# Taking a norm's root out of the matmul operand and multiplying it in on evacuation

## The reference, cut to what matters

```python
def rms_norm(x, w):
    return x * lax.rsqrt(jnp.mean(x * x, axis=-1, keepdims=True) + EPS) * w

def swiglu(x, w_gate, w_up, w_down):
    return (silu(x @ w_gate) * (x @ w_up)) @ w_down      # 1024 -> 2816 -> 1024

x = x + 0.5 * swiglu(rms_norm(x, ffn1_norm), ...)        # stage f1
h = rms_norm(x, mix_norm)
proj = h @ w_in                                          # conv inputs, gates, decay, q, k, v
x = x + concat([gdn_mixer(...), dilated_mixer(...)]) @ w_out
x = x + 0.5 * swiglu(rms_norm(x, ffn2_norm), ...)        # stage f2
x = rms_norm(x, final_norm)
```

## Time and profile before

| what | value |
|---|---|
| three runs | 2655.34, 2647.42, 2653.19 us; median 2653.19 us |
| the profiled execution | 2648.88 us, span 2647.0 us |
| PE matmul busy | 2557.2 us, 97% of the span |
| DVE busy | 1669.7 us, 63% |
| ACT busy | 1102.4 us, 42% |
| first block | about the first 665 us |

### The profile page before, as it was taken

One profiled execution on the slowest core, in us unless ns is written; L12 is line 12 of the kernel. 1 busy time (PEld: TensorE's weight loads), 2 busy tenths in 40 slices (PEclk: granted clock), 3 DMA queues, 4 the chain that ended last, 5 costly groups with the idle time before them and its releaser, 6 DMA issues.

```text
span 2647.0 us, 38421 instructions
## 1 busy us (share of the span) xinstructions
PE 2557.2 (97%) x15704; PEld 2268.5 (86%) x15704; DVE 1669.7 (63%) x2645; ACT 1102.4 (42%) x1728; POOL 64.4 (2%) x60
## 2 busy tenths in 40 slices
PE   7998898999999999999999999999999999998998
PEld 7998798999888888778888888889888888888998
DVE  6767644777677655666644767755555446776655
ACT  5445654555322223444243422224222225755553
POOL 0001031000000000000100000000000000000000
PEclk9999999999999999999999999999999999999999
DMA  7765201675455442212222455543444323244554
GB/s 261 233 231 184 88 17 62 208 240 185 167 180 185 168 150 97 66 40 80 94 90 88 143 187 177 176 163 111 145 140 134 135 98 126 89 138 149 179 189 148
DMA packets 109536, 379.92 MB, mean 144 GB/s; under 512 B 11952, under 2 KB 15792, under 8 KB 108976
## 3 DMA queue, kind: packets, MB, share of 16 engines
q1 hardware_dynamic: 108352, 372.80, 42.2%
q10 hardware_dynamic: 1008, 4.65, 0.5%
HBM read 376.36 MB, written 1.05 MB: 143 GB/s over the span
## 4 chain that ended last, share of the span: by engine, by line
PE 89%; DVE 5%; ACT 3%; issue 2%; DMA 0%; ACTq 0%; DVEq 0%
PE B L1499 26%; PE B L1501 26%; PE B L1500 26%; DVE w_lo L2129 2%; ACT w_hi L1820 1%; PE B L1760 1%; PE B L1743 1%; PE B L1514 1%; PE B L1653 1%; PE B L1515 1%; PE B L1516 1%; PE B L1666 1%; PE B L1750 1%; DVE AC L2374 1%; DVE TMP L2156 0%
## 5 line engine op out<-in xcount | busy, mean ns | idle before, releaser
L1499 PE MATMUL B<-U,w_hi 128*128 128x256 f32 (+1 forms) x2896 | 958.8, 331 | 7.9 <-DVE w_lo L2129 7.8
L1500 PE MATMUL B<-U,w_hi 128*128 128x256 f32 (+1 forms) x2896 | 950.7, 328 | 0.0
L1501 PE MATMUL B<-U,w_lo 128*128 128x256 f32 (+1 forms) x2896 | 950.5, 328 | 0.0
L2129 DVE TENSOR_TENSOR w_lo<-w_raw,w_hi 128x1024 fp32r<-128x1024 f32 (+3 forms) x583 | 683.2, 1184 | 385.6 <-ACT w_hi L1820 384.8
L1820 ACT ACTIVATE w_hi<-w_raw 128x1024 fp32r<-128x1024 f32 (+3 forms) x583 | 589.4, 1017 | 494.6 <-PE B L1501 471.9
L1499 PEld LDWEIGHTS B<-U,w_hi 128*128 128x128 f32 x2896 | 546.3, 189 | 64.4 <-issue 7.5
L1500 PEld LDWEIGHTS B<-U,w_hi 128*128 128x128 f32 x2896 | 546.1, 189 | 52.6 <-issue 1.5
L1501 PEld LDWEIGHTS B<-U,w_lo 128*128 128x128 f32 x2896 | 546.1, 189 | 51.6
L1499 PE MATMUL B<-HHf,w_hi 128*128 128x256 f32 (+1 forms) x1122 | 363.9, 324 | 1.5 <-DVE w_lo L2129 1.5
L1500 PE MATMUL B<-HLf,w_hi 128*128 128x256 f32 (+1 forms) x1122 | 363.0, 324 | 0.0
L1501 PE MATMUL B<-HHf,w_lo 128*128 128x256 f32 (+1 forms) x1122 | 363.0, 324 | 0.0
(11 more groups left out here) (360 smaller groups left out, 2510.1 us busy)
## 6 DMA issues: line engine op xcount, KB each, us to landing
w_raw<-in_w SPq DMA_DIRECT2D x504, 512.0 KB, 4.2
w_ada<-in_w SPq DMA_DIRECT2D x144, 512.0 KB, 3.3
w_raw<-in_w SPq DMA_DIRECT2D x58, 384.0 KB, 3.2
w_raw<-in_w SPq DMA_DIRECT2D x8, 320.0 KB, 2.8
X<-in_x SPq DMA_DIRECT2D x2, 1024.0 KB, 9.6
w_raw<-in_w SPq DMA_DIRECT2D x8, 256.0 KB, 2.7
BW<-in_bias ACTq DMA_DIRECT2D x1, 1536.0 KB, 10.2
CN<-in_consts ACTq DMA_DIRECT2D x1, 1152.0 KB, 5.3
```

The source lines that it names most:

```text
L1499: pe.matmul(o, hi, xh, start=i == 0 and s.start, stop=False)
L1500: pe.matmul(o, hi, xl, start=False, stop=False)
L1501: e = pe.matmul(o, lo, xh, start=False, stop=i == last and s.stop)
L2129: dve.tensor_tensor(w_lo[:, plan.slot[u], 0:n], w_raw[:, plan.ring[u], 0:n], w_hi[:, plan.slot[u], 0:n].bitcast(F32), ALU.subtract).then_i ...
```

## The change

In the first block no normed state is made. A step `raw` writes `hi` and `lo` of X times the norm's weight as soon as a chunk of X is final (at the start: as soon as it has landed), so the products read that. The root is one number for each token, so it can be multiplied in behind the products: on the gate bank ahead of silu (`g_r`), on the down product ahead of `x_add` (`x_r`; the up product is linear, so its root waits until there), on each bank of `mix1` as it is evacuated (`conv_in`, `gate_in`, `decay_tr`, `qk_sq`, now on VectorE), and for v, whose tokens lie on partitions, through a transposed root (`r_tr`) as the scale of ScalarE's copy. A `pair` behind a norm is cut in half, and the sum over partitions and the root stand between the halves. At the start X is loaded in two halves, with the first weight unit between them.

```diff
-                while done < min(at + AHEAD + 1, len(cut)) and ...
+                while done < min(at + (s.n if s.kind == "fetch" and s.n else AHEAD + 1), len(cut)) and ...
+    def raw(self, name, k, *need):
+        self.add("raw", key=(name, k), x=self.view, need=need)
+    def raw_begin(self, name, keys, wts, stat):
+        need = tuple(("ul", ("raw", name, k)) for k in range(8))
+        b, b2 = self.PS.get(), self.PS.get()
+        f = dict(x=self.view, n=256, need=need, b=b, b2=b2)
+        self.add("pair", key=(), wts=wts[:8], **f)
+        rb = stat.rsqrt(D)
+        self.add("pair", key=keys, wts=wts[8:], k0=4, **f)
+        self.lastU = ("mm", keys[1])
+        self.add("ahead")
+        return rb, dict(zip(keys, (b, b2)))
...                                                  # ffn, down part
-            self.x_add((p, "d", m), n, b, gate)
+            self.x_add((p, "d", m), n, b, gate, rb=rb)
             stat.add_("X", m, ("x_add", (p, "d", m)))
+            if raw:
+                self.raw(raw, m, ("x_add", (p, "d", m)), self.lastU)
...                                                  # whole, the start
+        wts = self.weights(self.first_of("f1"))
+        for k in range(4):
+            self.raw("ffn1_norm", k, ("x", 0))
+        self.add("fetch", u=wts[0][0], n=1)
+        for k in range(4, 8):
+            self.raw("ffn1_norm", k, ("x1", 0))
+        self.add("fetch", u=wts[-1][0])
         stat = Stat(self, "x", 256)
         for k in range(8):
-            stat.add_("X", k, ("x", 0))
-        rb = stat.rsqrt(D)
-        need = self.norm_to_u("ffn1_norm", rb, None)
+            stat.add_("X", k, ("x" if k < 4 else "x1", 0))
+        rb, begun = self.raw_begin("ffn1_norm", [("f1", "g", 0), ("f1", "u", 0)], wts, stat)
         self.add("cs")
+        stat = self.ffn("f1", 256, begun, None, (), raw="mix_norm", rb=rb)
...                                                  # mix1
-            yield split + (("P", 2750), ("A", 380))
+            yield split + (("P", 2750), ("D", 420))
+            self.raw("ffn2_norm", m, ("x_add", ("wout", m)), self.lastU)
...                                                  # scalar
+            elif k == "raw":
+                act.activation(HI[s.x][:, s.key[1], 0:256], X[:, s.key[1], 0:256], ACT.Copy,
+                               scale=col(*s.key))
             elif k == "ffn_h":
+                if s.rb:
+                    w.wait_ge(*at("g_r", s.key))
+                    act.activation(TM(s.t, s.n), TM(s.t, s.n), ACT.Silu)
-                act.activation(VB[:, s.key, :], PS(s.b), ACT.Copy)
+                act.activation(VB[:, s.key, :], PS(s.b), ACT.Copy, scale=SM(s.sm, s.key, s.key + 1))
...                                                  # vector
+            elif k == "raw":
+                w.wait_ge(*at("uh", ("raw", *s.key)))
+                dve.scalar_tensor_tensor(out=LO[...], in0=X[:, s.key[1], 0:256], scalar=col(*s.key),
+                                         in1=HI[...], op0=ALU.mult, op1=ALU.subtract)
+            elif k in ("conv_in", "gate_in"):
+                w.wait_ge(*at("mm", ("in", j)))
+                dve.tensor_tensor(o, PS(s.b, 256), RB(s.rb, 256), ALU.mult)
             elif k == "ffn_h":
+                if s.rb:
+                    w.wait_ge(*at("mm", (p, "g", j)))
+                    w.wait_ge(*at("st_exp", s.rb.name))
+                    dve.tensor_tensor(h, PS(s.b, s.n), RB(s.rb, s.n), ALU.mult)        # g_r
                 w.wait_ge(*at("silu", s.key))
                 w.wait_ge(*at("mm", (p, "u", j)))
                 dve.tensor_tensor(h, h, PS(s.b2, s.n), ALU.mult)
             elif k == "x_add":
+                if s.rb:
+                    dve.tensor_tensor(t, PS(s.b, s.n), RB(s.rb, s.n), ALU.mult)        # x_r
+                    dve.scalar_tensor_tensor(out=X[...], in0=t, scalar=0.5, in1=X[...], ...)
...                                                  # sync, before the other loads
-        sp.dma_start(X[:, :, 0:256], xs[:, :, 0:256])
+        sp.dma_start(X[:, 0:4, 0:256], xs[:, 0:4, 0:256])
         sp.dma_start(PC[:, 0:ncol], cols)
+        weight_in(plan.cut[0])
+        sp.dma_start(X[:, 4:8, 0:256], xs[:, 4:8, 0:256])
+        weight_in(plan.cut[1])
         sp.dma_start(C1[:], consts[:, 0:256])
```

More of the change, by code:

```diff
@@ L350, in seam, with x_add @@
         return second
-    def x_add(self, key, n, b, gate, o=0):
-        self.add("x_add", key=key, n=n, o=o, b=b, arg=gate)
+    def x_add(self, key, n, b, gate, o=0, rb=None):
+        t = self.TM.get() if rb else None
+        self.add("x_add", key=key, n=n, o=o, b=b, arg=gate, t=t, rb=rb)
+        if rb:
+            self.TM.done(t, ("x_add", key))
         self.PS.done(b, ("x_add", key))
@@ L408, in down, with ffn @@
         return [(p + "d", k, 128 * m, 128) for k in range(NF)]
-    def ffn(self, p, n, begun, gate, old, stat=None, beside=None):
+    def ffn(self, p, n, begun, gate, old, stat=None, beside=None, raw=None, rb=None):
         turns, share = 0, lambda i: min(i * ADA[p] // ADAS[p], ADA[p])
@@ L417, in ffn @@
             t = self.TM.get()
-            self.add("ffn_h", key=(p, j), n=n, b=g, b2=u, t=t, need=old)
-            self.PS.done(g, ("silu", (p, j)))
+            self.add("ffn_h", key=(p, j), n=n, b=g, b2=u, t=t, need=old, rb=rb)
+            self.PS.done(g, ("g_r" if rb else "silu", (p, j)))
             self.PS.done(u, ("hm", (p, j)))
@@ L513, in block2, with mix1 @@
             self.add("final2", key=k, rb=rb)
-    def mix1(self, wts, need):
+    def mix1(self, first, rb):
         self.add("mix1_load", need=(("mm", ("f1", "d", 7)),))
@@ L521, in mix1 @@
         PT = Ring(3)
-        first = self.pair([("in", 0), ("in", 1)], wts, 256, need)
+        sm = SM.get()
         done, silued, qk, kv, qn, vb = set(), set(), [], [], set(), []
@@ L528, in conv @@
                 yield from PS.room()
[L529 to L530 removed]
+            b = first["in", j] if j < 2 else self.gemm(("in", j), win(128 * j), 256)
+            self.add("conv_in", key=j, b=b, need=(old,), rb=rb)
             PS.done(b, ("conv_in", j))
[L532 removed]
+            yield split + (("P", 2750), ("D", 420))
             self.add("conv_taps", key=j, need=(old,))
@@ L619, in attn_qk @@
             t, t2 = TM.get(), TM.get()
-            self.add("qk_sq", key=j, b=b, t=t)
-            yield split + (("P", 2750), ("A", 400))
+            self.add("qk_sq", key=j, b=b, t=t, rb=rb, need=(old,))
+            PS.done(b, ("qk_r", j))
+            yield split + (("P", 2750), ("D", 420), ("A", 400))
             yield from PS.room()
@@ L634, in attn_v @@
         def attn_v():
-            yield from PS.room(2)
+            yield from PS.room(3)
+            b = PS.get()
+            self.add("r_tr", b=b, sm=sm, rb=rb)
+            PS.done(b, ("r_col", 0))
             b, b2 = PS.get(), PS.get()
@@ L782, in mix1 @@
             pass
+        self.RB.done(rb, ("gate_in", 3), ("conv_in", 11), ("qk_r", 7), ("decay_f", 0))
         def finish(c):
@@ L1709, in tensor @@
                 pe.matmul(PS(s.b, s.n), ones, TM(s.t, s.n), start=True, stop=True).then_inc(*up("ln_mm", l))
+            elif k == "r_tr":
+                w.wait_ge(*at("st_exp", s.rb.name))
+                w.each(s.b.after)
+                for i in range(2):
+                    e = pe.transpose(hs(PS(s.b), i), hs(RB(s.rb), i), ident)
+                e.then_inc(*up("r_tr", 0))
             elif k == "rk_tr":
@@ L1865, in scalar @@
                 act.activation(r[0], r[0], ACT.Exp, scale=-0.5).then_inc(*up("st_r1", s.key))
-            elif k == "norm":
-                w.wait_ge(*at("nt", s.key))
-                w.each(e for e in s.need if e)
-                act.activation(HI[s.x][:, s.key[1], 0:s.n], TM(s.t, s.n), ACT.Copy).then_inc(*up("uh", s.key))
+            elif k == "raw":
+                w.wait_ge(*at("cols", 0))
+                w.each(s.need)
+                act.activation(HI[s.x][:, s.key[1], 0:256], X[:, s.key[1], 0:256], ACT.Copy,
+                               scale=col(*s.key)).then_inc(*up("uh", ("raw", *s.key)))
             elif k in ("anorm", "fnorm"):
@@ L2166, in vector @@
                 h = TM(s.t, s.n)
+                if s.rb:
+                    w.wait_ge(*at("mm", (p, "g", j)))
+                    w.wait_ge(*at("st_exp", s.rb.name))
+                    w.each(s.t.after)
+                    dve.tensor_tensor(h, PS(s.b, s.n), RB(s.rb, s.n), ALU.mult).then_inc(*up("g_r", s.key))
                 w.wait_ge(*at("silu", s.key))
```

127 lines of the change are left out of this document (58 added, 69 removed).

## The result

The changed kernel takes 2692.41 us (median of 4 runs, 2686.12 to 2694.37) against 2650.99 before (4 runs on the same chip, 2647.42 to 2655.34): ratio 1.014, 95% interval 1.0115 to 1.0166. Forecast were 2663 and a range of 2643 to 2675. The direction was right, the size was not: slower by 41 us instead of 9.5.

What follows compares the result with a forecast made beforehand. TensorE was taken to bound the kernel, with VectorE becoming the bound in f1 and f2 turns. Terms 5.4 + 0.55 + 1.1 - 6.8 + 4 - 3.9 + 9.1 = +9.5 us gave 2663 us, range 2643 to 2675.

Steps and rivals of the forecast that it cites:

- the term of `mix1`: `mix1`: 25 evacuations become VectorE multiplies at 0.33 us each; between a gain of 3 and a loss of 8.3, taken +4.
- The recorded sign that `mix1` moves by more than 9 us: `mix1`: a move of more than 9 us was stated beforehand as showing the prediction wrong.
- Rival C: f1 and f2: TensorE's waits let the clock fall, four falls costing 6.6 us; +20 in all, 2674 us, chance 0.12.
- The lane: f1 and f2 turns: VectorE needs 5.01 us, 6.71 with a `w_ada` row; its mean exceeds TensorE's 5.44.
- in f2: f2 with its down part: TensorE waits on VectorE behind `w_ada` rows, +9.1 us.
- Start and f1: Start to the down part of f1: earlier start included, VectorE's late `g_r` decides, +5.4 us.
- The down turns: Down part of f1: +1.1 us from waits at three rows, and 0.55 from the last row's delay.
- The seams: Seams before `mix1` and before f2: shorter by 6.8 us and 3.9 us.
- Rival A: f1 and f2: added handoffs cost under 0.5 to 0.6 us a turn, VectorE stays under TensorE; 2644 us, chance 0.17.

Runs made afterwards that it cites:

- e6: Kernel of e1 with the 8 q and k products not multiplied by the root, ScalarE squaring them out of PSUM; 2664.65 us, ratio 1.0032.
- e12: Kernel before the change with the 8 q and k products copied out of PSUM by VectorE, ScalarE squaring the copy; 2669.35 us, ratio 1.0056.
- e8: Kernel before the change with 12 conv and 4 gate evacuations as copies on VectorE instead of ScalarE; 2656.28 us, ratio 1.0003.
- e5: Kernel of e1 with the three `mix1` constant transfers issued earlier, behind f1's last raw hi; 2672.89 us, ratio 1.0075.
- e1: Changed kernel with the old planner costs, so `mix1` has the step order of before the change; 2675.72 us, ratio 1.01.
- e3: Changed kernel with all 24 `w_ada` rows of f1 and f2 taken in f2, none in f1; 2694.94 us, ratio 1.0172.
- e4: Changed kernel with the same instructions of f1 and f2 turns interleaved in another order on VectorE and ScalarE; 2673.55 us, ratio 1.0087.
- e2: Kernel before the change with only the new planner costs, so `mix1` has the changed kernel's step order; 2662.93 us, ratio 1.0051.
- e10: Kernel of e9 with the changed kernel's planner costs for conv, gate and decay, q and k charged to ScalarE; 2654.75 us, ratio 1.0006.
- e9: Changed kernel with the edits of e1, e4, e5 and e6 together; 2652.65 us, ratio 0.9991.
- e7: Kernel of e1 with the conv and gate multiplies issued later, just ahead of the taps; 2680.81 us, ratio 1.0097.
- e11: Changed kernel in its own order, with only q and k left without the root; 2683.65 us, ratio 1.0109.

## Why the prediction was wrong

**The failed step** is the term of `mix1`: "Bounds: a gain of 3 ... and a loss of all 8.3", of which I took +4; measured +27. The recorded sign that `mix1` moves by more than 9 us came true. The term fell in three ways.

- *The price of a moved evacuation.* I priced it by its busy time and took 25 times that for the upper bound. The busy time was right (9.1 us more). But an evacuation on a chain costs the time that it stands in the new engine's queue, and what waits in order behind its reader. Eight on the chain product, square, sum, root, band cost 12.8 us (e6) and 13.5 (e12), 1.6 to 1.7 us each, some 5 us of each sum through the lower clock; sixteen beside it 3.8 (e8). The rows were there: VectorE at 68% in this stretch, with w_lo units of over a microsecond each. I used the share to say where TensorE stands and not how long a newcomer queues.
- *The order.* I named the new plan only as a possible gain. It is a loss of 7.7 us on top of the multiplies and 14.5 alone. Its costs were true to the change and the order still was worse; why is open (below).
- *The constants.* The forecast named what the seams free and not what is late next. ScalarE still issued the three transfers of `mix1` at the head of that stage, and the stage now began earlier against them: CB was issued 3.9 us ahead of the first qk gemm before (206.98, 210.84) and 0.7 behind it after (214.86, 214.17). The sum of squares met it: 3.4 us, 3.7 of the stretch (e5).

These make 12.8 + 3.8 + 3.7 = 20.3 against the 19.3 of e1, as near as single profiles allow; 7.7 more for the order make the 27.0 measured.

**Rival C was partly right, in another place.** I gave 6.6 us to a falling clock, in f1 and f2. There the waits stayed short, and the mean stays at 1.00 in f1; in `mix1` it went from 0.97 to 0.86, and TensorE's 16.8 us of added busy time are over half of the loss, where I had given the clock nothing in `mix1`. The Trainium skill ("TensorE: Matmul & The Clock Gate", "A second HAM failure mode: psum-queue depth-cycling") says that frequent short idle times can make the clock swing; this trace agrees for `mix1`, where the clock fell seven times, with waits up to 3.4 us, against three times before. No run shows what each fall followed from, and what part of the loss would remain at a steady clock wasn't tried.

**What held.** The lane: 5.04 and 6.71 us, +9.2 in f2 against +9.1, and e3 and e4 move it as the argument says. Start and f1 came to +7.8 instead of +5.4: `g_r` (0) stood at 26.25 (forecast 26.0), but `g_r` (1) at 31.64 and not 29.9, and the lane kept that (`g_r` (19) at 134.04 instead of 132.0). The second gate gemm started at 23.75, not 21.5; it varies, 20.9 (e1) to 23.75 in the profiles with this start. The down turns +1.9 against 1.65. The seams -6.35 against -6.8, and -2.8 against -3.9. An evacuation's own time is 0.420 us on VectorE and 0.381 to 0.384 on ScalarE, 36 to 39 ns more. The Trainium skill ("Perfetto Trace Analysis", "Optimizing Scalar/DVE Operations") gives 125 against 51 ns of access overhead on PSUM, 74 ns apart. The trace agrees in the sign; the measured difference is half of that, and it is one of whole durations, which hold more than this overhead. Either number explains 1 to 2 of the 27 us.

**Rival A's condition was the right one** (handoffs out of VectorE's way), and e4 met it by hand: 15.4 us back in f1 and f2. It needed an order of work that the change did not bring.

**Open.** Which swap in the new order costs the 14.5 us of e2, and why its loss is mostly clock, is not settled. e10 narrows it: with the new costs for conv, gate and decay, but q and k charged to ScalarE alone, `mix1` is only 2.3 us longer than in e9. That points at the cost written for q and k; it was not tried by itself. e7 mixes two edits.

## What to carry to other kernels

Before an evacuation is moved to another engine, ask whether somebody waits for it. On a chain it costs the queue ahead of it on the new engine: here ScalarE stood 1.9 us longer for each (e12), and 1.7 us of that came out in the stretch, for an operation of 0.4. Beside the chain the same move cost 0.2 us. When a stage starts earlier, list all that it needs and check that each issue moves with it, the constants too. And when costs of a planner change, run its new order alone: that takes one run, and here it told 14 us apart that otherwise would have been laid on the instructions.

## What the runs showed of the hardware that was not expected

In these traces a train of gemms without any wait runs at one of two paces while the granted clock is 1.00. The same part of f21, before and after:

```profile
2500.00:2550.00 50.00, 50.00 (x444) 50.00 (x443) 30.52 (x37) 24.73 (x38) 0.00 (x0) 1.00 0.56 193
```

```profile
2510.00:2560.00 50.00, 50.00 (x426) 50.00 (x426) 29.48 (x36) 23.41 (x37) 0.00 (x0) 1.00 0.58 190
```

444 matmuls in 50 us or 426; a gemm of 24 takes 2.72 or 2.83 us. f21 has the slower pace in the profiles of after, e1, e2, e7, e8, e11 and e12, and not in those of before, e3 to e6, e9 and e10. Kernels with and without the change are on both sides, so the 6.5 us that f21 seemed to lose are not tied to it. The median of after, 2692.41, probably holds them too: its profile does, and its fastest run is 2686.12. Without them the change costs some 37 us and not 43.6 (an estimate, the sum of the other rows). In e9 the pace fell on f1 and f2. In f1 and f2 of the kernel after, it changes only at waits, in either direction. What chooses it was not found. For comparisons it means that one profile against another is uncertain by 4.5 us (f1, f2) to 6.5 us (f21) for each such train, and that a difference is better read per stretch than from the total.
